# One product of the last expert unit ahead of another, and router logits of three token tiles on column strips

## The reference, cut to what matters

```
h = _layer_norm(DN_ALPHA * h + y, ln_w[layer, 0], ln_b[layer, 0])
y = _moe(h, router_w, moe_w_gate[layer], moe_w_up[layer], moe_w_down[layer])

probs = softmax(x @ router_w)                     # 512 x 16 logits
# one of 4 groups per token, and the top 2 of its 4 experts
hid = silu(xblk @ w_gate[e]) * (xblk @ w_up[e])   # 1024 -> 512
y_e = hid @ w_down[e]                             # 512 -> 1024
```

## Time and profile before

| | us |
|---|---|
| median of three runs | 1321.58 (1319.5 to 1322.45) |
| the profiled execution | 1323.91 |
| its span, first to last instruction | 1322.0 |
| PE busy | 1242.3 (94%) |
| DVE busy | 519.5 (39%) |
| ACT busy | 186.1 (14%) |
| POOL busy | 166.6 (13%) |

### The profile page before, as it was taken

The page is one execution under the profiler, slowest core; times in us unless marked ns, Lnnn a source line. Parts: engine busy times, 40 slices in busy tenths (PEclk is TensorE's granted clock), DMA queues, the critical chain, the costliest instruction groups (busy, mean ns, idle before and its releaser), DMA issues.

```text
span 1322.0 us, 13922 instructions
## 1 busy us (share of the span) xinstructions
PE 1242.3 (94%) x5523; PEld 577.8 (44%) x5523; DVE 519.5 (39%) x1010; ACT 186.1 (14%) x313; POOL 166.6 (13%) x126
## 2 busy tenths in 40 slices
PE   8999999987999997899999999999899879999965
PEld 4444464632333332344555555555446323333322
DVE  1352792461211110620455666656725612111108
ACT  0016400110000000111111111111112100000000
POOL 0000400023000000100122332223300230000010
PEclk9999999987999998899999999999999989999988
DMA  9930075079999999353220122200064699999983
GB/s 353 366 116 0 0 319 222 15 298 380 397 429 427 427 427 420 154 142 127 64 64 24 41 64 64 63 0 0 0 263 188 280 395 403 427 426 427 426 336 149
DMA packets 82849, 301.51 MB, mean 228 GB/s; under 512 B 6405, under 2 KB 50793, under 8 KB 70377
## 3 DMA queue, kind: packets, MB, share of 16 engines
q1 hardware_dynamic: 61312, 262.55, 50.0%
q10 hardware_dynamic: 16872, 21.38, 4.5%
q0 software_dynamic: 4608, 16.78, 3.3%
HBM read 269.23 MB, written 31.46 MB: 227 GB/s over the span
## 4 chain that ended last, share of the span: by engine, by line
PE 84%; DVE 6%; DMA 5%; issue 3%; POOL 1%; ACT 1%; SPq 0%; DVEq 0%; POOLq 0%
PE ps L633 18%; PE ps L800 14%; PE ps L496 11%; PE ps L668 10%; PE ps L573 8%; PE ps L787 4%; PE ps L822 4%; PE ps L852 2%; PE ps L609 1%; DMA W<-moe_w_gate 1%; PE ps L688 1%; DVE S L1670 1%; PE ps L565 1%; POOL slot_rows L1767 1%; PE ps L840 1%
## 5 line engine op out<-in xcount | busy, mean ns | idle before, releaser
L633 PE MATMUL ps<-W,S 128*32 128x512 f32 (+1 forms) x1200 | 276.7, 604 | 6.5 <-DMA W<-moe_w_gate 5.0
L800 PE MATMUL ps<-hT,W 128*128 128x512 f32 x512 | 232.5, 593 | 0.7 <-ACT W L931 0.7
L633 PE MATMUL ps<-S 128*32 128x512 f32 (+1 forms) x592 | 142.3, 604 | 5.9 <-DMA W<-moe_w_gate 5.9
L633 PEld LDWEIGHTS ps<-W,S 128*32 128x32 f32 (+1 forms) x1200 | 82.1, 125 | 131.5 <-issue 128.7
L800 PEld LDWEIGHTS ps<-hT,W 128*128 128x128 f32 x512 | 92.8, 191 | 90.4 <-issue 88.5
L668 PE MATMUL ps<-W,hT 128*64 128x512 f32 (+1 forms) x512 | 123.9, 602 | 8.7 <-issue 6.8
L668 PE MATMUL ps<-S,hT 128*32 128x512 f32 (+1 forms) x384 | 95.5, 604 | 8.3 <-issue 8.3
L1801 POOL TENSOR_TENSOR W<-S,sq 128x256 f32<-128x256 f32 x64 | 73.5, 1148 | 160.7 <-PE ps L822 117.1
L931 ACT ACTIVATE hT<-ps 128x512 f32<-128x512 f32 x68 | 39.0, 598 | 357.5 <-PE ps L668 250.7
L496 PE MATMUL ps<-W,hT 128*128 128x512 f32 x192 | 86.5, 610 | 1.7 <-DMA W<-w_in_even 1.7
L1712 DVE TENSOR_TENSOR S<-S 128x512 f32<-128x512 f32 x64 | 47.8, 747 | 69.7 <-PE ps L822 57.9
(11 more groups left out here) (260 smaller groups left out, 1321.8 us busy)
## 6 DMA issues: line engine op xcount, KB each, us to landing
W<-moe_w_gate SPq DMA_DIRECT2D x24, 2048.0 KB, 17.5
W<-moe_w_up SPq DMA_DIRECT2D x21, 2048.0 KB, 21.7
W<-moe_w_down SPq DMA_DIRECT2D x20, 2048.0 KB, 23.2
S<-moe_w_down SPq DMA_DIRECT2D x12, 2048.0 KB, 23.0
S<-moe_w_up SPq DMA_DIRECT2D x11, 2048.0 KB, 22.1
S<-moe_w_gate SPq DMA_DIRECT2D x8, 2048.0 KB, 17.9
W<-w_in_odd SPq DMA_DIRECT2D x32, 512.0 KB, 6.4
slot_rows<-S ACTq DMA_DIRECT2D x4, 2816.0 KB, 19.5
```

The source lines that it names most:

```text
L633: last = pe.matmul(ps[a:a + n, bank, :], xgT[:, c, a:a + n], home(kind, p)[:, c, :], start=(c == 0), stop=(c == ND - 1))
L800: last = pe.matmul(ps[:, f % 2, :], ring[slot][:, f, c, :], hT[:, c, :], start=(c == 0), stop=(c == ND - 1))
```

## The change

Three things move. In the last unit up(9) is issued ahead of down(8). The logits of tiles 0 to 2 are computed together: eight matmuls, one per chunk of `hT`, each with 32 columns of `rw` stationary on one of the four column strips of PE and 384 tokens streaming (`logit_parts`). ACT copies the four partial sums (128x384) to `parts`, and three small matmuls with a constant 0/1 matrix `fold` as the moving operand add them up and turn them to 16 logits per token (`fold_parts`). The constant is one more transfer at the start, and POOL clears one more 128x16 block there. The counts of the semaphores follow.

```diff
+            def logit_parts(L):
+                pe.wait_ge(hT_done, (2 * L + 1) * 2 * NT + 2 * (NT - 1))
+                pe.wait_ge(prmC, 2 * L + 2)
+                for c in range(ND):
+                    a = c % 4 * STRIP
+                    last = pe.matmul(ps[a:a + STRIP, 1, 0:(NT - 1) * P], view(rw[:], c * NE, [[1, STRIP]]),
+                                     hT[:, c, 0:(NT - 1) * P], start=(c < 4), stop=(c >= 4))
+                last.then_inc(logits_ps, 1)
+            def fold_parts(L):
+                pe.wait_ge(prmC, 2 * L + 3)
+                for t in range(NT - 1):
+                    last = pe.matmul(ps[:, 0, t * NE:(t + 1) * NE], parts[:, t * P:(t + 1) * P], fold[:],
+                                     start=True, stop=True)
+                last.then_inc(logits_ps, 1)
...
             def last_logits(L):
-                logits(L, 2, range(4, ND))
                 turn_h(2 * L + 1, NT - 1, (1,))
...
                 gate(LAST)
+                up(LAST)
                 down(LAST - 1)
-                up(LAST)
...
                     out_project(k, mixT, w_out0, range(4), True, False)
-                    logits(0, 1)
+                    logit_parts(0)
                     turn_h(1, NT - 1, (0,))
-                    logits(0, 2, range(4))
                     out_project(k, mixT, w_out0, range(4, ND), False, True).then_inc(op_ps, 1)
+                    fold_parts(0)
                 if k == 5:
                     turn_h(1, 0)
                 if k == 6:
                     turn_h(1, 1)
                     turn_h(1, 2)
-                    logits(0, 0)
...
+            def copy_parts(L):
+                act.wait_ge(logits_ps, 3 * L + 1)
+                copy(parts, ps[:, 1, 0:(NT - 1) * P]).then_inc(prmC, 1)
...
-            for t in range(1, NT):
-                turn_copies(1, t)
+            turn_copies(1, 1)
+            turn_copies(1, 2)
+            copy_parts(0)
+            turn_copies(1, 3)
...
-            for half in range(2):
-                scale_output(3, (half,))
-                turn_copies(3, 3, (half,))
+            scale_output(3, (0,))
+            copy_parts(1)
+            turn_copies(3, 3, (0,))
+            scale_output(3, (1,))
+            turn_copies(3, 3, (1,))
...
             def scaled_logits(L, t):
-                dve.wait_ge(logits_ps, L * NT + max(t + 1, NT - 1))
+                dve.wait_ge(logits_ps, 3 * L + (2 if t < NT - 1 else 3))
```

More of the change, by code:

```diff
@@ L114, in constants @@
                                           [STRIP * FIRST_STRIP[p] for p in BY_RANK]]).astype(f)[None, :], (P, 1)),
+        "c_fold": (j[:, None] % STRIP == np.arange(NE)[None, :]).astype(f),
     }
@@ L120, in encoder_kernel @@
                    router_w, moe_w_gate, moe_w_up, moe_w_down,
-                   c_rot, c_decay, c_masks, c_sq, c_iota, out):
+                   c_rot, c_decay, c_masks, c_sq, c_iota, c_fold, out):
     with ExitStack() as ctx:
@@ L134, in encoder_kernel @@
         sq = sb("sq", [P, 3, P])
-        rw = sb("rw", [P, ND, NE])
+        rw = sb("rw", [P, ND + 1, NE])
+        fold = sb("fold", [P, NE])
         prm = sb("prm", [P, NROWS])
@@ L210, in encoder_kernel @@
         first_sel = S3(12288, NT, P)
+        parts = S[:, 13312:13312 + (NT - 1) * P]
         xgT = S3(15360, ND, P)
@@ L500, in _ @@
                 project(n)
-            pe.wait_ge(prm_in, 16 * 10)
+            pe.wait_ge(prm_in, 16 * 11)
             pe.transpose(ps[:, 0, 0:NROWS], prm_rows[0:NROWS], ident[0:NROWS, 0:NROWS]
@@ L514, in router_spread @@
             def router_spread(L, bank):
-                pe.wait_ge(prmC, L + 2)
+                pe.wait_ge(prmC, 2 * L + 2)
                 pe.matmul(ps[:, bank, 2 * NE:4 * NE], ones[0:2, :], terms[0:2, 2:4, :].rearrange("p a e -> p (a e)"),
@@ L578, in logits @@
                 pe.wait_ge(hT_done, (2 * L + 1) * 2 * NT + 2 * t + (1 if chunks[-1] < ND // 2 else 2))
-                pe.wait_ge(prmC, L + 2)
                 for c in chunks:
-                    last = pe.matmul(ps[:, 0 if t < NT - 1 else 2, t * NE:(t + 1) * NE], hT[:, c, t * P:(t + 1) * P], rw[:, c, :],
+                    last = pe.matmul(ps[:, 2, t * NE:(t + 1) * NE], hT[:, c, t * P:(t + 1) * P], rw[:, c, :],
                                      start=(c == 0), stop=(c == ND - 1))
@@ L911, in _ @@
                     out_project(k, OG, w_out1, range(4), True, False)
-                    logits(1, 1)
+                    logit_parts(1)
                     turn_h(3, NT - 1, (0,))
-                    logits(1, 2, range(4))
                     out_project(k, OG, w_out1, range(4, HG), False, True).then_inc(op_ps, 1)
+                    fold_parts(1)
                 if k == 5:
@@ L920, in _ @@
                     turn_h(3, 2)
-                    logits(1, 0)
             last_logits(1)
@@ L952, in _ @@
             act.dma_start(rot[:], c_rot.rearrange("(n p) a k -> p n a k", p=P)).then_inc(tab_in, 16)
-            act.dma_start(rw[:], router_w.rearrange(rows, p=P)).then_inc(tab_in, 16)
+            act.dma_start(rw[:, 0:ND, :], router_w.rearrange(rows, p=P)).then_inc(tab_in, 16)
             act.dma_start(iota[:], c_iota).then_inc(tab_in, 16)
+            act.dma_start(fold[:], c_fold).then_inc(prm_in, 16)
             def projected(n):
@@ L1039, in moe @@
                 if L == 0:
-                    act.wait_ge(logits_ps, NT)
-                    act.dma_start(rw[:], router_w.rearrange(rows, p=P)).then_inc(tab_in, 16)
+                    act.wait_ge(logits_ps, 3)
+                    act.dma_start(rw[:, 0:ND, :], router_w.rearrange(rows, p=P)).then_inc(tab_in, 16)
                 ysb = xs.rearrange("(b p) d -> b p d", p=P)
@@ L1226, in router_terms @@
                                 view(ident[0:2], 0, [[1, 2], [0, NE]]), ALU.mult)
-                v.tensor_tensor(rw[:], rw[:], view(prm[:], R_LNW + ND * L, [[1, ND], [0, NE]]), ALU.mult).then_inc(prmC, 1)
+                v.tensor_tensor(rw[:, 0:ND, :], rw[:, 0:ND, :], view(prm[:], R_LNW + ND * L, [[1, ND], [0, NE]]), ALU.mult
+                                ).then_inc(prmC, 1)
             def spread_terms(L):
@@ L1746, in _ @@
         def _(pool):
+            pool.memset(rw[:, ND:ND + 1, :], 0.0)
             pool.memset(zero, 0.0).then_inc(zero_set, 1)
```

## The result

| | before | changed |
|---|---|---|
| median, us | 1321.66 (5 runs) | 1314.82 (1311.71 to 1315.77, 5 runs) |
| ratio, 95% interval | | 0.9942 (0.9931 to 0.9954) |
| the profiled execution, us | 1323.91 | 1315.77 |
| its span, us | 1322.0 | 1313.9 |
| PE busy, us | 1242.3 | 1233.0 |

The kernel is faster by 6.8 us between the medians of these runs, 7.7 by the ratio. The prediction was 1317.7, a gain of 3.9. Later runs of the same code gave 1314.15 beside 1322.31 of before, ratio 0.9936 (0.9920 to 0.9951): 8.2 us between the medians, 8.5 by the ratio.

The account below looks back on a forecast made before the run. PE, 84% of the chain of waits, was taken as the bound. Logits gain 5.24 us, the new order loses 1.32: 3.92 us less, from 1321.58 to 1317.7 us, range 1315.2 to 1321.5.

Parts of the forecast that it names:

- Logits, 2.62 us per layer: At the out projection, strip logits start the second half of k = 7 2.62 us sooner per layer, 5.24 in all.
- their cover: Fold matmuls, 0.64 us, lie in PE's 0.95 us wait for DVE; ACT's copy, at most 0.60, delays nobody.
- 1.65 was forecast: Ahead of the second half of k = 7: strips 1.29 us plus switching tiling mode, 0.26 in and 0.1 out.
- the 79%: Share of full strip overlap by a skill rule; eight strip matmuls would take 1.63 us instead of the 1.29 taken.
- The wait split in two: Behind gate(9), PE waits for up(9)'s weights 1.5 us in the first layer, 3.3 in the second; none ahead of down(8).
- The clock, -1.6 us: Second layer's 3.3 us wait ahead of up(9) loses the full clock, costing 1.6 us; no loss in the first layer.
- The first rival: The clock holds in the second layer's wait, so none of the 1.6 is lost: 1316.1 us; chance 18%.
- The end of down(8), +0.55 and -0.27 us: At full clock, down(8) ends 0.55 us sooner in the first layer and 0.27 later in the second.
- The end of the layer moves only as far as the end of down(8) moves: Behind the last units, the chain goes from down(8)'s end to store and gather, so only its shift (+0.55, -0.27) counts.
- the gather's 8.79 us: First layer's chain behind down(8): 6.69 us at the store of unit 8's rows, 8.79 at the first tile's gather.
- The prediction's third rival: Transfers, not the scatter, set when the experts end, so the logits' gain doesn't arrive: 1322.9 us; chance 9%.
- the offset of 2.33 us: The profiled execution before was 2.33 us above the median of the runs, so the forecast starts from 1321.58.

Follow-up runs that it names:

- e2: Kernel before with only up(9) put ahead of down(8), logits as before: 1321.5 us, ratio 0.9998.
- e13: Changed kernel plus 29 matmuls of 16 columns on PE in the first layer's wait ahead of the first sums: 1316.85 us, one run.
- e9: Changed kernel plus 7.9 us of extra matmuls on PE ahead of down(8) in the first layer: 1320.23 us, ratio 0.9981.
- e6: Changed kernel plus 2.8 us of extra matmuls on PE ahead of down(8) in the second layer: 1317.32 us, ratio 0.9963.
- e1: Changed kernel with the old order of the last unit, so the logits' strips alone: 1316.77 us, ratio 0.9955.
- e3: Changed kernel with up(9) ahead of down(8) in the first layer only: 1316.31 us, ratio 0.9957.
- e4: Changed kernel with up(9) ahead of down(8) in the second layer only: 1315.43 us, ratio 0.9952.
- e5: Changed kernel plus 2.8 us of extra matmuls on PE ahead of down(8) in the first layer: 1316.7 us, ratio 0.9957.
- e10: Changed kernel with the two w_in_odd loads issued only once the first tile's gathered rows have landed: 1312.2 us, ratio 0.9922.
- e14: e10 plus 3 matmuls of 128x384 between gate(9) and up(9): 1310.33 us, ratio 0.9915.
- e15: e14 with the w_in_odd loads waiting for the second tile's rows instead of the first's: 1310.0 us, ratio 0.9914.

## Why the prediction was wrong, and where it was right

**Logits, 2.62 us per layer: right.** 2.57 and 2.54 us at the two places, and the fold and the copy stayed under their cover, as forecast. The eight strip matmuls took 1.50 us by their records. The transposes behind them start 1.64 us after their start, but 0.06 us after DVE's addition (253.79 + 0.68), so it is DVE that sets this place and 1.64 is only the most that strips and switching can have taken; 1.65 was forecast. By the 79% that the prediction worked out from the Trainium skill (TensorE: Matmul & The Clock Gate, Part 3) it would be an estimated 1.99; the trace does not agree.

**The wait split in two: right in kind, wrong in both sizes.** 1.5 us in the first layer was 2.4, and 3.3 in the second was 2.4, because the weights' landing was taken from one run, and gate(9)'s end against the landing is a difference of large numbers. Over the runs it was 2.1 to 2.7 in the first layer and 1.9 to 3.5 in the second.

**The clock, -1.6 us: the failed term in the second layer.** The step that failed is the length of the wait, and the loss with it: 2.39 us, in which the clock held, and up(9) took 7.09. The first rival came true there. For a wait as long as the forecast had it, the loss was right: both that were above 3.3 us lost 1.69. So the loss was a fair price for a profile with the packet in the scatter, as the one of before is. Without the packet none of eight waits in this layer lost the clock. What a loss costs at the end is open: e2's profile has 0.8 us more than the others, e13's nothing.

**The end of down(8), +0.55 and -0.27 us.** From gate(9)'s end it comes after 15.9 to 16.0 us in the first layer with the old order and 16.1 to 16.4 with the new one while the clock holds, 18.1 to 18.3 where it is lost. In the second it is 16.1 to 16.9 with the old and 15.9 to 16.9 with the new. So the order moved it by next to nothing, and the 0.55 us was not there to be passed on.

**"The end of the layer moves only as far as the end of down(8) moves": wrong in the first layer.** The prediction took the gather's 8.79 us as a price of the path, and it was for a large part a wait for the queues: 5.35 in e9. So the lost clock there, 1.69 us, cost nothing either. In the second layer the step holds in part: of e6's 3 us later store 1.1 arrive. The prediction's third rival had this mechanism and put it at the wrong end, against the logits' gain; but since the fetches start behind the scatter, the backlog itself moves with the logits, and their gain arrives in full.

**What no step had: 1.0 us in the second layer's scatter**, shown by e13's profile.

The sum with these sizes: 2.57 + 2.54 + 1.0 + 0 + 0.4 = 6.5 us. Against the forecast's 3.9 the second layer's order makes up 2.3 us of the difference (+0.4 for -0.27 - 1.6), the scatter 1.0, the first layer's order -0.55 and the logits -0.1. That the 0.4 belongs to the order is not shown. Measured were 6.8 and 8.2 between the medians, 7.7 and 8.5 by the ratios. The logits with the scatter alone, 6.1, stand against e1's 5.3 (medians) and 5.9 (ratio). The rest of the profile's 8.15 us I put down to phase. 0.81 us are PE's eight cumulative-sum matmuls ahead of the first scatter, 1.81 us before and 1.00 in all others, e2 with the old logits among them:

```profile
269.42 1.00 PE L600 MATMUL ps<-S,sq 128*128 128x64 f32 x8
```

0.42 was there when the runs reached the place of the change, and 0.5 is the spread of the distance 237.2 to 238.7. The forecast had taken the offset of 2.33 us between that execution of before and the median off as a whole, and that was fair.

What stays open: whether the order in the second layer is worth 0.4 us in time (it is read from distances in single profiles, and e1, e3 and e4 don't separate) and why, whether e5's 2.8 us are hidden in every run or only where the clock holds ahead of them (with a loss its store would be at 222.5, the edge of what is free), and the remaining 0.3 to 2 us between the sum and what was measured.

## What to carry to other kernels

A transfer's duration in the chain of waits is not a price until it is known what else is in the queues: if they are full, ask when the backlog ends and who started it, and treat the two limits as a maximum. Before counting a step as gain or loss, put work in front of it: once by the size of the doubt and once by more, so that both limits show. Loads that nobody needs yet, issued ahead of a gather that the end waits for, can cost more than the order of two products: here 2 us by the medians of e10, 2 to 4 by the ratios of e10, e14 and e15, against 0.4 at most. A wait read from one profile holds for that profile: ask what else fell into it before carrying its length, and a loss of clock that hangs on it, over to the changed kernel.

## What the runs showed of the hardware

One packet of 16 KB on the instruction queue took 0.92 us of one DMA engine, and the scatter with it 7.9 to 9.4 us after its start (before, e2, e13) had its last row written 0.9 to 1.1 us later than without it. The last slices at a sixteenth of the rate suggest that the scatter is spread over all sixteen engines and done when the slowest is. At 1.2 to 3.4 us after the start of the first layer's scatter, which ends at 13.46 to 13.48 us without such a packet, it cost 0 to 0.14 us; why so little was not tested.

Waits of equal length lose the clock or keep it: 2.41 us lost it and 2.39 kept it in the same execution. A loss was 1.69 us each of five times (8.78 against 7.09 us for the 32 records).
